# Decay, forget and write-strength rows from sixteen cumulated rows and a 0/1 product, rectifier on ScalarE

## The chip, the cores and the metric

The kernel runs on one core of one Trainium2 chip. The metric is the device time of one execution in microseconds (us), the median of several runs. A time in a trace is counted from the start of the profiled execution's span. PE is TensorE, DVE VectorE, ACT ScalarE, POOL GpSimd, and SP the engine that issues the weight loads.

## What is computed

Two transformer blocks for 256 tokens of width 1024, one after the other. The change lies in the second one, whose mixer has four heads of a gated delta rule (GDN, head size 128) and eight heads of a "forgetting" attention (FoX). Cut to what matters:

```python
proj = rmsnorm(h) @ w_in
g_qkv, g_z, g_a, g_b, f_qkv, f_f = split(proj)
g_qkv = silu(causal_depthwise_conv(g_qkv, conv_w))       # 12 tiles of 128 features: q, k, v of 4 heads
gq, gk = l2norm(gq), l2norm(gk)
beta = sigmoid(g_b)                                      # write strength, (tokens, 4)
g_decay = -exp(a_log) * softplus(g_a + dt_bias)          # log decay, (tokens, 4)
# gated_delta_rule, by chunks:
gc = cumsum(g_decay)
decay = where(lower, exp(gc[i] - gc[j]), 0)
a_mat = where(strict, (k * beta) @ k.T * decay, 0) + eye # then a triangular solve
# forgetting_attention:
log_f = log_sigmoid(f_f + fox_f_bias)                    # (tokens, 8)
c = cumsum(log_f)
logits = q @ k.T * scale + c[i] - c[j]                   # causal softmax over j, times v
```

## The kernel before

**Tiling and weights.** Every large product is made of three products of fp32r parts (high times high, high times low, low times high). Weights stream in groups of 1 MB through a ring of three: SP loads `raw`, ACT rounds it to `w_hi` (`hi_until`, L668), DVE subtracts to `w_lo` (`lo_until`, L1275), PE uses both. A group of the ring is rounded when PE has used the group three before it. Each engine has its own instruction stream, written out by hand in the order in which it runs, and the streams meet in counting semaphores: `wait_ge` on one of them holds everything behind it on that engine.

**The stage of the change.** For j = 0 to 5, `gdn_tiles(j)` on PE makes two tiles of 128 features for 256 tokens (48 matmuls of 256 columns). ACT moves them out of PSUM with the middle tap (`gdn_mid`, L987), DVE adds the other three taps (`gdn`, L1668, six instructions), ACT does the silu (`gdn_silu`, L995), PE turns four heads at a time to tokens (`to_tokens`, L2112). Tiles 0 and 1 are the queries, 2 and 3 the keys, 4 and 5 the values. ACT squares the turned rows (`token_squares`, L1017), DVE sums them, POOL makes the root (L605, L606) and DVE the normed `qk_n` (`token_norms`, L1711). PE turns these back (`gT`, moved out by ACT, L1066) and forms the products kk of keys with keys and queries (L2562).

**What the change touches.** DVE makes `g_dec`, `beta` and `lf2` (log forget) for each token (L1687 to L1694). PE then has, behind `gdn_tiles(2)`:

- `decay_sums` (L2483): the cumulated decay `gc` as columns (L2488, L2489), and for each of 2 token tiles and 4 heads a 128x128 product of the head's `g_dec`, broadcast as the stationary operand, with the triangle `s_le_t` (L2492). Each gives the cumulated row, the same on all partitions.
- `forget_sums(i)` (L2496), i = 0 to 3, each for two of the eight FoX heads: six such 128x128 products into bank 7 (L2506 to L2508), moved out negated to `neg_c` by ACT's `fsum_out(i)` (L1009). All these products are plain fp32.
- behind the flips of `qk_n`: eight products that spread `beta` over the partitions (L2552).

DVE subtracts `gc` from the decay rows and cuts at zero (`decT`, L1723, eight instructions), ACT takes the exponential (L1040). `egc` (L1729, L1043) holds exponentials of `gc` columns. DVE multiplies kk by `decT` and by the spread `beta` to `cT` (L1748, L1751), and the triangular solve starts from `cT`.

## Time and profile before

| | us |
|---|---|
| median of 3 runs | 809.65 |
| lowest, highest | 808.44, 810.8 |
| profiled execution | 811.04 |
| its span (first to last instruction) | 809.1 |
| PE busy in the span | 776.0 (96%) |
| DVE busy | 540.3 (67%) |
| ACT busy | 414.6 (51%) |
| POOL busy | 93.3 (12%) |

How to read it: a busy share is an average over stages. A row of the timeline gives the start, the length of the merged instructions, the engine, the line of the kernel, the operation and its tiles, how many instructions it merges, and in brackets the time that the engine sat idle before it and who ended that. A matmul's length includes its way through the array, so matmuls overlap: what one costs PE is the distance between starts. A plain fp32 matmul shows as two entries (x16 for eight).

### The profile page before, as it was taken

Reading aid. Unit: us, or ns where it says so; the run is one execution under the profiler, and the core shown is the slowest. Engines: PE = TensorE matmul, PEld = TensorE weight load, DVE = VectorE, ACT = ScalarE, POOL = GpSimd, SP = SyncE. Lnnn points to the kernel's source line nnn. Section 1 sums busy time; section 2 is a strip of 40 time slices with the busy share of each in tenths; the row PEclk is TensorE's granted clock in tenths of the full one; section 3 lists DMA queues with packets and bytes.
Section 4 is the critical chain, followed back from the end, with each engine's and each line's share of the span. In section 5 each row is a group of like instructions: output and inputs, shape, how many; then the busy total and the mean of one; then the engine's idle time right before and its main releaser. Section 6 shows DMA issues by size and latency. Waiting matters only on the chain. (4 is left out here: it accounts for less than half of the span.)

```text
span 809.1 us, 11764 instructions
## 1 busy us (share of the span) xinstructions
PE 776.0 (96%) x4591; PEld 665.5 (82%) x4591; DVE 540.3 (67%) x713; ACT 414.6 (51%) x581; POOL 93.3 (12%) x154
## 2 busy tenths in 40 slices
PE   4899999999999999999989999999999999999996
PEld 3777877777889899888889988988788898988884
DVE  0676789876777888877577885564466666654365
ACT  2632422634676776634267545556365454543364
POOL 3100401311200000000170313210100000000000
PEclk9999999999999999999999999999999999999998
DMA  9976576814276555588454343312465555545711
GB/s 307 362 251 222 196 247 228 301 54 143 79 234 207 184 176 181 188 275 301 150 141 150 104 157 103 105 55 66 143 233 173 192 193 172 206 157 185 232 53 53
DMA packets 107900, 144.83 MB, mean 179 GB/s; under 512 B 6343, under 2 KB 70352, under 8 KB 107856
## 3 DMA queue, kind: packets, MB, share of 16 engines
q1 hardware_dynamic: 100512, 137.38, 51.1%
q10 hardware_dynamic: 7280, 6.83, 2.7%
q8 instruction: 30, 0.49, 0.2%
q14 instruction: 14, 0.11, 0.0%
q0 software_dynamic: 64, 0.01, 0.0%
HBM read 142.10 MB, written 2.10 MB: 178 GB/s over the span
## 5 line engine op out<-in xcount | busy, mean ns | idle before, releaser
L2072 PE MATMUL ps<-h_parts,w_hi 128*128 128x512 f32 x504 | 179.6, 396 | 0.0
L1275 DVE TENSOR_TENSOR w_lo<-raw,w_hi 128x2048 fp32r<-128x2048 f32 (+1 forms) x61 | 135.6, 2230 | 63.4 <-ACT w_hi L668 63.2
L668 ACT CAST w_hi<-raw 128x2048 fp32r<-128x2048 f32 (+1 forms) x61 | 112.9, 1852 | 80.6 <-PE ps L1948 56.8
L2071 PE MATMUL ps<-h_parts,w_lo 128*128 128x256 f32 x504 | 140.5, 279 | 0.0
L1283 DVE TENSOR_TENSOR w_lo<-raw,w_hi 128x2048 fp32r<-128x2048 f32 x44 | 100.7, 2290 | 16.2 <-ACT w_hi L676 15.7
L2072 PEld LDWEIGHTS ps<-h_parts,w_hi 128*128 128x128 f32 x504 | 94.6, 188 | 19.4
L2071 PEld LDWEIGHTS ps<-h_parts,w_lo 128*128 128x128 f32 x504 | 95.0, 189 | 3.3
L676 ACT CAST w_hi<-raw 128x2048 fp32r<-128x2048 f32 x44 | 84.0, 1909 | 0.0
L1946 PE MATMUL ps<-w_hi,act_hi 128*128 128x512 f32 x176 | 69.0, 392 | 0.0
L1948 PE MATMUL ps<-w_hi,act_lo 128*128 128x512 f32 x176 | 68.5, 389 | 0.0
L1947 PE MATMUL ps<-w_lo,act_hi 128*128 128x512 f32 x176 | 68.5, 389 | 0.0
L1946 PE MATMUL ps<-w_hi,h_parts 128*128 128x512 f32 x160 | 64.2, 401 | 1.2 <-DVE h_parts L1301 0.7
L1948 PE MATMUL ps<-w_hi,h_parts 128*128 128x512 f32 x160 | 62.4, 390 | 0.0
L1947 PE MATMUL ps<-w_lo,h_parts 128*128 128x512 f32 x160 | 62.3, 390 | 0.0
L1946 PE MATMUL ps<-h_parts,w_hi 128*128 128x256 f32 x144 | 41.4, 287 | 0.0
L1947 PE MATMUL ps<-h_parts,w_hi 128*128 128x256 f32 x144 | 40.7, 283 | 0.0
L1948 PE MATMUL ps<-h_parts,w_lo 128*128 128x256 f32 x144 | 40.7, 283 | 0.0
L1947 PEld LDWEIGHTS ps<-w_lo,act_hi 128*128 128x128 f32 x176 | 33.0, 188 | 7.1 <-issue 0.2
L1946 PEld LDWEIGHTS ps<-w_hi,act_hi 128*128 128x128 f32 x176 | 33.0, 188 | 6.9 <-issue 0.2
L1948 PEld LDWEIGHTS ps<-w_hi,act_lo 128*128 128x128 f32 x176 | 33.0, 188 | 6.9
L1946 PEld LDWEIGHTS ps<-w_hi,h_parts 128*128 128x128 f32 x160 | 30.0, 188 | 9.6 <-DVE h_parts L1301 1.6
L498 POOL TENSOR_SCALAR ss<-ss 128x1 f32<-128x1 f32 x14 | 5.5, 396 | 278.4 <-ACT junk L686 278.4
(418 smaller groups left out, 1548.7 us busy)
## 6 DMA issues: line engine op xcount, KB each, us to landing
raw<-in_ffn_up_w SPq DMA_DIRECT2D x22, 1024.0 KB, 5.1
raw<-in_w_gate_up SPq DMA_DIRECT2D x22, 1024.0 KB, 5.1
raw<-in_ada_w SPq DMA_DIRECT2D x16, 1024.0 KB, 5.2
raw<-in_w_in SPq DMA_DIRECT2D x14, 1024.0 KB, 5.3
raw<-in_m_in_w SPq DMA_DIRECT2D x11, 1024.0 KB, 5.2
raw<-in_ffn_down_w SPq DMA_DIRECT2D x10, 1024.0 KB, 5.2
raw<-in_w_down SPq DMA_DIRECT2D x10, 1024.0 KB, 5.0
raw<-in_m_out_w SPq DMA_DIRECT2D x4, 1024.0 KB, 5.2
```

The lines of the kernel that those rows point to most:

```text
L498: link(pool.tensor_scalar(s, s, ss[:, c0 + TT:c0 + TT + 1], EPS, ALU.add, ALU.add))
L668: act.copy(part_view(w_hi, s), raw_view(split[s])).then_inc(hi_ready, 1)
L676: act.copy(part_view(w_hi, s), raw_view(split[s])).then_inc(hi_ready, 1)
L1275: dve.tensor_tensor(part_view(w_lo, s), raw_view(split[s]), part_view(w_hi, s).bitcast(F32), ALU.subtract).then_inc(lo_ready, 1)
L1283: dve.tensor_tensor(part_view(w_lo, s), raw_view(split[s]), part_view(w_hi, s).bitcast(F32), ALU.subtract).then_inc(lo_ready, 1)
L1946: pe.matmul(dst, l_hi, r_hi, start=first, stop=False)
L1947: pe.matmul(dst, l_hi, r_lo, start=False, stop=False)
L1948: return pe.matmul(dst, l_lo, r_hi, start=False, stop=last)
L2071: pe.matmul(both[:, 0], lo[:, k, w], h_hi[:, k, :], start=False, stop=False)
L2072: ins = pe.matmul(both, hi[:, k, w], h_parts[:, :, k, :], start=False, stop=k == KD - 1)
```

## The change

The three gates of a token become one tile of sixteen columns, `token_gates`: eight of log forget, four of decay, four of beta. `gate_sums` cumulates all sixteen at once with the columns as the stationary operand, so that they come out as sixteen rows over 256 tokens (3 products), and turns the same columns without cumulating them (2 transposes), into 16 partitions of bank 7. ACT copies these rows to fp32r (`gate_sum` 0 to 15), DVE subtracts to the rest of the rounding (`gate_sum` 32 to 47), in the memory of `mw`, which is not used any more by then. A row is spread over the 128 partitions by `spread`: a 0/1 column of `pick`, broadcast as the stationary operand, with `gate_sum`, one fp32r product of 256 columns. `decay_spread` (four, and the two of forget group 0) stands in the middle of `gdn_tiles(3)`, the other forget groups and beta where they were. The bank layout of the decay and beta rows changes from one bank for each token tile to two heads in each bank. The subtraction of `gc` and the cut at zero move from DVE to ACT as a rectifier of `gc` minus the row; the exponential takes it with the scale −1. `fsum_out(1)` moves up on ACT, `gdn(2)` on DVE stands now ahead of the wait for `egc_exp`, and DVE gains a copy of `fold` to `pick`.

ACT, from the move of gdn 2's tiles out of PSUM on (`r<-ps,cols`); before:

```order
L987 ACTIVATE r<-ps,cols 128x256 x2
L710 COPY p_out<-ps 128x512 x2
L712 DMA out<-p_out 128x2x512
L1040 ACT_TABLE_LOAD
L1040 ACTIVATE decT<-decT 128x512 x2
L1043 ACTIVATE egc<-egc 128x4 x2
L995 ACT_TABLE_LOAD
L995 ACTIVATE r<-r 128x256 x4
L1009 ACTIVATE neg_c<-ps 128x512
L668 CAST w_hi<-raw 128x2048
```

and now (here L991 is gdn_mid, L999 the silu, L1013 neg_c, L672 w_hi):

```order
L991 ACTIVATE r<-ps,cols 128x256 x2
L1041 CAST mw<-ps 16x512
L714 COPY p_out<-ps 128x512 x2
L716 DMA out<-p_out 128x2x512
L1047 ACTIVATE decT<-ps,gc 128x128 x8
L1053 ACT_TABLE_LOAD
L1053 ACTIVATE decT<-decT 128x512 x2
L1056 ACTIVATE egc<-egc 128x4 x2
L999 ACT_TABLE_LOAD
L999 ACTIVATE r<-r 128x256 x4
L1013 ACTIVATE neg_c<-ps 128x512
L672 CAST w_hi<-raw 128x2048
```

The copy of the rows and the eight rectifiers are new; the table load for the exponential stands behind the rectifiers.

PE, behind the last matmuls of gdn 2's tiles, with the first of gdn 3's; before:

```order
L1948 MATMUL ps<-h_parts,w_lo 128x256
L2488 MATMUL ps<-g_dec,s_le_t 128x4 x2
L2489 MATMUL ps<-g_dec,ones 128x4
L2492 MATMUL ps<-s_le_t,g_dec 128x128 x8
L2506 MATMUL ps<-s_le_t,lf 128x128
L2507 MATMUL ps<-ones,lf 128x128
L2508 MATMUL ps<-s_le_t,lf 128x128
L2506 MATMUL ps<-s_le_t,lf 128x128
L2507 MATMUL ps<-ones,lf 128x128
L2508 MATMUL ps<-s_le_t,lf 128x128
L1946 MATMUL ps<-h_parts,w_hi 128x256
```

and now, with, in the middle of gdn 3's tiles, the spreads (`ps<-mw,pick`):

```order
L1958 MATMUL ps<-h_parts,w_lo 128x256
L2501 MATMUL ps<-token_gates,s_le_t 128x4 x2
L2502 MATMUL ps<-token_gates,ones 128x4
L2505 MATMUL ps<-s_le_t,token_gates 16x128 x2
L2506 MATMUL ps<-ones,token_gates 8x128
L2122 MATMUL ps<-ident,token_gates 16x128 x2
L1956 MATMUL ps<-h_parts,w_hi 128x256
...
L1958 MATMUL ps<-h_parts,w_lo 128x256
L2494 MATMUL ps<-mw,pick 128x256 x6
L1956 MATMUL ps<-h_parts,w_hi 128x256
```

Fourteen products of 128 columns gave way to five, and six spreads moved into the tiles.

The diff:

```diff
         mw = sb(ctx, "mw", [64, 2, 2, T], F32R)
+        pick = sb(ctx, "pick", [64, 16], F32R)
+        gate_sum = mw[:, 0].rearrange("p d t -> p (d t)")
...
             gprm = sb(b2, "gprm", [P, 16])
-            g_dec = sb(b2, "g_dec", [P, TT, GH])
-            beta = sb(b2, "beta", [P, TT, GH])
-            lf2 = sb(b2, "lf2", [P, TT, FH])
+            token_gates = sb(b2, "token_gates", [P, TT, 16])
+            lf2, g_dec, beta = (token_gates[:, :, c0:c1] for c0, c1 in ((0, FH), (FH, FH + GH), (FH + GH, 16)))
             sp2 = sb(b2, "sp2", [P, TT, 16])
...
             return j % 2 if j >= 2 else 6 + j
+
+        def by_head_and_tile(b):
+            return ps[:, b:b + 2, :].rearrange("p b (u t n) -> p (b u) t n", u=2, t=TT)
...
             gdn_mid(2, ahead=False)
+            act.wait_ge(S("sgate_ready"), 3)
+            act.copy(gate_sum[0:16], ps[0:16, 7, :]).then_inc(S("sgate_ready"), 1)
             p_store(1)
+            act.wait_ge(S("egc_diff"), 2)
+            act.wait_ge(S("decay_mm"), 2)
+            for t in range(TT):
+                for h in range(GH):
+                    ins = act.activation(decT[:, GH * t + h, :], by_head_and_tile(5)[:, h, t, :], ACT.Relu, scale=-1.0,
+                                         bias=gc[:, t, h:h + 1])
+                ins.then_inc(S("dec_z"), 1)
             for t in range(TT):
...
                 d = decT[:, GH * t:GH * (t + 1), :]
-                act.activation(d, d, ACT.Exp).then_inc(S("dec_exp"), 1)
+                act.activation(d, d, ACT.Exp, scale=-1.0).then_inc(S("dec_exp"), 1)
             act.wait_ge(S("egc_diff"), 2)
...
             gdn_mid(3)
+            fsum_out(1)
             gdn_silu(3)
...
             token_squares(1)
-            fsum_out(1)
             gdn_mid(4, ahead=False)
...
+            dve.wait_ge(S("const_ready"), 3)
+            link(dve.tensor_copy(pick[:], fold[0:64]))
             gdn(1)
...
             dve.tensor_tensor(egc[:, 2, :], gc[:, 2, :], gc[:, 0, :], ALU.subtract).then_inc(S("egc_diff"), 1)
-            for t in range(TT):
-                dve.wait_ge(S("decay_mm"), 1 + t + 1)
-                for h in range(GH):
-                    ins = dve.tensor_scalar(decT[:, GH * t + h, :], ps[:, 5 + t, h * P:(h + 1) * P], gc[:, t, h:h + 1], 0.0,
-                                            ALU.subtract, ALU.min)
-                    if h < GH - 1:
-                        link(ins)
-                ins.then_inc(S("dec_z"), 1)
+            dve.wait_ge(S("sgate_ready"), 4)
+            dve.tensor_tensor(gate_sum[32:48], ps[0:16, 7, :], gate_sum[0:16].bitcast(F32), ALU.subtract).then_inc(S("sgate_ready"), 1)
+            gdn(2)
             dve.wait_ge(S("egc_exp"), 2)
             dve.tensor_tensor(egc[:, 1, :], egc[:, 0, :], beta[:, 1, :], ALU.mult).then_inc(S("egc_ready"), 1)
-            gdn(2)
             gdn(3)
...
                 link(dve.tensor_tensor(all_heads(cT, t), bank(4 + t), all_heads(decT, t), ALU.mult))
+            dve.wait_ge(S("beta_mm"), 1)
             for t in range(TT):
-                dve.wait_ge(S("beta_mm"), t + 1)
-                dve.tensor_tensor(all_heads(cT, t), all_heads(cT, t), bank(2 + t), ALU.mult).then_inc(S("cT_full"), 1)
+                dve.tensor_tensor(all_heads(cT, t), all_heads(cT, t), by_head_and_tile(2)[:, :, t, :], ALU.mult)\
+                    .then_inc(S("cT_full"), 1)
...
-            def decay_sums():
-
-                pe.wait_ge(S("sgate_ready"), 1)
+            def spread(dst, c, rows):
+                return pe.matmul(dst, pick[:, c:c + 1].to_broadcast([64, P]), rows, start=True, stop=True)
+
+            def gate_sums():
+
+                pe.wait_ge(S("sgate_ready"), 2)
                 pe.wait_ge(S("conv2_done"), 2)
...
                 pe.matmul(ps[:, 4, 8:12], ones[:], g_dec[:, 0, :], start=True, stop=True).then_inc(S("decay_mm"), 1)
+                pe.wait_ge(S("conv2_done"), 4)
                 for t in range(TT):
-                    for h in range(GH):
-                        ins = pe.matmul(ps[:, 5 + t, h * P:(h + 1) * P], g_dec[:, t, h:h + 1].to_broadcast([P, P]),
-                                        s_le_t[:], start=True, stop=True)
-                    ins.then_inc(S("decay_mm"), 1)
-
-            def forget_sums(i):
-
-                if i == 0:
-                    pe.wait_ge(S("sgate_ready"), 2)
-                    pe.wait_ge(S("conv2_done"), 4)
-                else:
+                    pe.matmul(ps[0:16, 7, t * P:(t + 1) * P], token_gates[:, t, :], s_le_t[:], start=True, stop=t == 0)
+                pe.matmul(ps[0:FH, 7, P:T], lf2[:, 0, :], ones[:], start=False, stop=True)
+                for t in range(TT):
+                    ins = flip(ps[0:16, 7, T + t * P:T + (t + 1) * P], token_gates[:, t, :])
+                ins.then_inc(S("sgate_ready"), 1)
+
+            def decay_spread():
+
+                pe.wait_ge(S("sgate_ready"), 5)
+                for h in range(GH):
+                    ins = spread(ps[:, 5 + h // 2, h % 2 * T:(h % 2 + 1) * T], FH + h, gate_sum[:, 0:T])
+                ins.then_inc(S("decay_mm"), 1)
+                forget_spread(0)
+
+            def forget_spread(i):
+
+                if i:
                     pe.wait_ge(S("neg_c_out"), i)
                 for b in range(2):
-                    f0, f1 = (lf2[:, t, 2 * i + b:2 * i + b + 1].to_broadcast([P, P]) for t in range(TT))
-                    c = b * T
-                    pe.matmul(ps[:, 7, c:c + P], f0, s_le_t[:], start=True, stop=True)
-                    pe.matmul(ps[:, 7, c + P:c + T], f0, ones[:], start=True, stop=False)
-                    ins = pe.matmul(ps[:, 7, c + P:c + T], f1, s_le_t[:], start=False, stop=True)
+                    ins = spread(ps[:, 7, b * T:(b + 1) * T], 2 * i + b, gate_sum[:, 0:T])
                 ins.then_inc(S("fsum_mm"), 1)
...
             gdn_tiles(2)
-            decay_sums()
-            forget_sums(0)
-            gdn_tiles(3)
+            gate_sums()
+            gdn_tiles(3, between=decay_spread)
             pe.wait_ge(S("dec_z"), TT)
...
             to_tokens(0, 1, TOKEN_BANKS[1])
-            forget_sums(1)
+            forget_spread(1)
             gdn_tiles(4)
-            forget_sums(2)
+            forget_spread(2)
             to_tokens(1, 0, TOKEN_BANKS[2])
...
             to_tokens(1, 1, TOKEN_BANKS[3])
-            forget_sums(3)
+            forget_spread(3)
             gdn_tiles(5)
...
-            for t in range(TT):
-                for h in range(GH):
-                    ins = pe.matmul(ps[:, 2 + t, h * P:(h + 1) * P], beta[:, t, h:h + 1].to_broadcast([P, P]), ident[:],
-                                    start=True, stop=True)
-                ins.then_inc(S("beta_mm"), 1)
+            for h in range(GH):
+                ins = spread(ps[:, 2 + h // 2, h % 2 * T:(h % 2 + 1) * T], FH + GH + h, gate_sum[:, T:2 * T])
+            ins.then_inc(S("beta_mm"), 1)
             fox_tiles(0)
```

## Rows read from the trace of the kernel before

**Rows 1.** The page: busy us (share of the span) x instructions of each engine.

```profile
PE 776.0 (96%) x4591; PEld 665.5 (82%) x4591; DVE 540.3 (67%) x713; ACT 414.6 (51%) x581; POOL 93.3 (12%) x154
```

**Rows 2.** Timeline of PE, 424 to 454.5 us: start, length, engine, line, operation.

```profile
431.92 0.51 PE L2488 MATMUL ps<-g_dec,s_le_t 128*128 128x4 f32 x4
...
432.51 2.03 PE L2492 MATMUL ps<-s_le_t,g_dec 128*128 128x128 f32 x16
434.38 0.39 PE L2506 MATMUL ps<-s_le_t,lf 128*128 128x128 f32 x2
...
435.64 0.36 PE L1946 MATMUL ps<-h_parts,w_hi 128*128 128x256 f32 x1
...
441.56 1.06 PE L2112 MATMUL ps<-ident,r 128*128 128x128 f32 x8
...
443.72 0.36 PE L1946 MATMUL ps<-h_parts,w_hi 128*128 128x256 f32 x1
...
450.83 0.49 PE L2506 MATMUL ps<-s_le_t,lf 128*128 128x128 f32 x2 [1.12 <-ACT neg_c L1009]
```

**Rows 3.** Timeline of ACT, 424 to 492 us.

```profile
434.39 1.28 ACT L1040 ACT_TABLE_LOAD   x1 [0.46 <-ACT p_out L710]
436.53 0.63 ACT L1040 ACTIVATE decT<-decT 128x512 f32<-128x512 f32 x1 [0.86 <-DVE decT L1723]
437.95 0.63 ACT L1040 ACTIVATE decT<-decT 128x512 f32<-128x512 f32 x1 [0.78 <-DVE decT L1723]
438.48 0.28 ACT L1043 ACTIVATE egc<-egc 128x4 f32<-128x4 f32 x2
438.79 1.28 ACT L995 ACT_TABLE_LOAD   x1
440.08 1.34 ACT L995 ACTIVATE r<-r 128x256 f32<-128x256 f32 x4
441.32 0.58 ACT L1009 ACTIVATE neg_c<-ps 128x512 f32<-128x512 f32 x1
441.80 1.89 ACT L668 CAST w_hi<-raw 128x2048 fp32r<-128x2048 f32 x1
...
468.13 2.03 ACT L1066 COPY gT<-ps 128x512 f32<-128x512 f32 x4
```

**Rows 4.** Timeline of DVE, 424 to 492 us.

```profile
429.58 2.95 DVE L1668 SCALAR_TENSOR_TENSOR r<-ps,cols,r 128x255 f32<-128x255 f32 x6 [0.27 <-ACT r L987]
...
434.99 2.92 DVE L1723 TENSOR_SCALAR decT<-ps,gc 128x128 f32<-128x128 f32 x8
...
443.72 2.29 DVE L1275 TENSOR_TENSOR w_lo<-raw,w_hi 128x2048 fp32r<-128x2048 f32 x1 [1.90 <-ACT w_hi L668]
445.93 2.94 DVE L1668 SCALAR_TENSOR_TENSOR r<-ps,cols,r 128x255 f32<-128x255 f32 x6
...
459.17 0.69 DVE L1711 TENSOR_TENSOR qk_n<-ps,rstd 128x512 f32<-128x512 f32 x1 [0.68 <-POOL rstd L606]
...
464.83 2.94 DVE L1668 SCALAR_TENSOR_TENSOR r<-ps,cols,r 128x255 f32<-128x255 f32 x6
```

**Rows 5.** Timeline of PE, 454.5 to 492 us.

```profile
460.32 1.91 PE L2112 MATMUL ps<-ident,qk_n 128*128 128x128 f32 x16
462.07 1.95 PE L2552 MATMUL ps<-ident,beta 128*128 128x128 f32 x16
...
470.21 3.84 PE L2562 MATMUL ps<-gT 128*128 128x128 f32 x32 [0.45 <-ACT gT L1066]
...
484.95 0.50 PE L1946 MATMUL ps<-w_hi,h_parts 128*128 128x512 f32 x1 [0.48 <-DVE vb L1766]
```

**Rows 6.** Timeline of ACT, 775 to 787 us.

```profile
775.76 2.17 ACT L1204 ACTIVATE h_parts<-ps,cols 128x128 fp32r<-128x128 f32 x8
```

**Rows 7.** Busy time by stretch at the end, with the granted clock (PEclk, 1.00 is 2.4 GHz).

```profile
803.00:804.00 1.00, 0.00 (x0) 0.00 (x0) 0.97 (x2) 0.60 (x2) 0.00 (x0) 1.00 0.17 62
804.00:805.00 1.00, 0.00 (x0) 0.00 (x0) 0.10 (x1) 0.12 (x2) 0.69 (x2) 0.65 0.00 0
```


## What I predict before the changed kernel runs

> **What bounds the kernel now.** I read first the page's busy shares [rows 1]: PE is busy 96% of the span. A reader who stops there will credit every removed matmul in full. So I read next, in time order, what each engine does between 430 and 485 us, where all of the change lies.
>
> PE [rows 2]: behind the tiles of gdn 2 it computes the decay sums and four groups of "forget" sums without a gap. But it meets its operands very closely. It starts the turned keys and queries (L2112) at 441.56, and the silu that makes them ends between 440.08 and 441.4 on ACT [rows 3]. It starts the flips of qk_n at 460.32 [rows 5], and the last qk_n is made by 459.86 on DVE [rows 4]. It waits 0.45 us for gT at 470.21 and 0.48 us for vb at 484.95 [rows 5]. So in this stage PE and the pair ACT and DVE run side by side with about 0.1 to 0.5 us between them: the end follows whichever is later.
>
> ACT [rows 3]: waits for decT from DVE at 436.53 and 437.95, two Exps, a table load, four Silus, one neg_c, and at 441.80 the high part of weight group 5 (w_hi, L668, 1.89 us). DVE [rows 4] waits for exactly this: 1.90 us idle before 443.72. From there DVE goes on almost by itself: low part, convolution 3 (445.93), the norms, ending in qk_n at 459.86, convolutions 4 and 5 (464.83), and ACT's gT (468.13), on which PE waits at 470.21. Its own gaps on the way are waits on POOL for rstd, which starts from DVE's own sums. So this chain is rigid: what delays w_hi 5 delays kk at 470.21, and all that follows.
>
> **The change part by part, in the time of the profiled execution** (811.04 us, span 809.1; the median of the three runs is 809.65, 1.39 lower; I carry the shift over to it unchanged).
>
> PE, removed: eight decay products, 432.51 to 434.38, 1.87 us; four forget groups of six, each 434.38 to 435.64 and some 0.08 more before the stride is back to normal, 1.34 us each, 5.4 in all; eight beta products, 1.8 [rows 2, 5]. Together 9.0 us. Added: three products of 128 moving columns at the 0.225 of the forget products (1.34/6) and two transposes at 0.11 (eight from 441.56 to 442.46), 0.9 us; sixteen spreads of 256 columns, which are of the type and width of the tiles' matmuls: 48 of these fill 435.64 to 441.56, 0.123 each, 2.0 us. Also removed is the wait of 1.12 at 450.83, since fsum_out(1) moves ahead. So PE has 6.1 us less work and up to 1.1 less waiting. That is the tempting sum: 809.65 − 7.2 = 802.4. It needs PE to be the bound all along.
>
> ACT, the new path. The three gc products still end at 432.51. The rows' products then wait for both convolutions of gdn 1, on DVE from 429.58 for 2.95 [rows 4]: 432.6. With 0.9 of products, gdn 3's tiles start at 433.5 (before: 435.64). The pick copy on DVE (64x16) falls into the 0.27 us that DVE idles before 429.58 and costs nothing; without this cover it costs its 0.17. ACT copies the sums (16x512; neg_c, a copy of 128x512, takes 0.5) at 433.6, then p_out and its DMA issue, as before with room to spare (they were through at 434.36, when gdn 2's tiles had ended at 432), and is idle by 436. DVE's subtraction (0.69, as qk_n's at 459.17) starts where decT started, 434.99, and ends at 435.7. PE comes to the spreads after half of gdn 3's tiles, 433.5 + 24 x 0.123 = 436.45, so neither is late, by 0.7 us. Four decay spreads and the drain: 437.15. This is where ACT's wait ends, and behind that wait everything else of ACT is queued.
>
> From 437.15: eight rectifiers of 128x128 from PSUM with an operand per partition. Nearest row: eight of this size with a scale per partition in 2.17 us, 0.27 each [rows 6]. Bounds: the two 128x4 Exps of 0.28 together [rows 3] with the slope of larger ones give some 0.2 each; DVE's own price for this work, 2.92 for eight, 0.365 each [rows 4]. So 1.6 to 2.9, and I take 2.2, ending at 439.35. Then the table load, 1.28: in the kernel before it was issued at 434.39 and lay under the wait for decT; now it stands behind the rectifiers, whose result the Exp wants: 440.65. Two Exps (0.63, overlapping) 441.8; egc 442.0; table load 443.3; four Silus (440.07 to 441.32 before, 1.25) 444.55; neg_c 0.48: w_hi 5 starts at 445.05, against 441.80 [rows 3]. **ACT is 3.25 us late**. DVE loses its 2.92 us of decT and does convolution 2 early, but only waits the longer for w_hi 5: nothing of that saving is on this path.
>
> DVE then starts w_lo 5 at 446.95 instead of 443.72, adds egc·beta (0.16), now ahead of convolution 3: +3.4. On the rigid chain this gives qk_n at 463.3, gT and kk at 473.6 instead of 470.21. The beta saving (1.3 us) falls into PE's wait for gT and is lost.
>
> PE, checked on this timetable: it finishes gdn 3's tiles and spreads at 440.15 and then waits for the Silus until 444.55, 4.4 us. It starts gdn 4 at 445.75 (before 443.72), ends at 451.6, waits about 1 us for silu 3 (449.3 before, 452.9 now), ends gdn 5 at 461 and waits 2.2 us for qk_n. The 7.2 us come back as these waits and that for gT. **Sum: +3.4 us**, 812.5 of span, 814.4 in a profiled execution, 813.05 on the median. With the bounds of the rectifiers (−0.6, +0.7) and some 0.3 on the spreads and semaphores: 812.1 to 814.1.
>
> Two rules of the pages beside that. Eight rectifiers took 0.365 each on DVE [rows 4] and should take 0.27 on ACT [rows 6]; the Trainium skill, page ScalarE: Activation LUTs, section Rules for kernel authors, says to put relu on VectorE and not on ScalarE. Per instruction this case's rows don't bear it out; what costs here is the queue that they stand in. Its section What ACT_TABLE_LOAD costs gives, besides the 1.28, 1.38 us of drain for each switch; in the trace the load at 438.79 starts 0.03 us after the end of egc's Exps, and the Silus follow it [rows 3]. I see no drain; with one the load now on the path would add 1.4, 814.4. It also says that cheap functions such as relu are in every set, which agrees with the order of the new kernel, where no load stands ahead of the rectifiers.
>
> **The rivals.**
> Faster: the late chain finds slack that I don't see, and PE's work sets the end. Then PE counts +2.0 at gdn 4, −1.1 and −1.1 for forget groups 2 and 3, −1.1 for the wait at 450.83 and −1.3 for beta: −2.6, 807.05. It speaks for it that PE did not wait at 460.32. It decides once the chain from 443.72 to 470.21 can shorten by 6 us; DVE's gaps on it are waits on POOL, and gT was already late by 0.45 [rows 5].
> Same: ACT's path costs a microsecond less than summed (rectifiers at their lower bound, and shorter gaps at the semaphores): +2.3 or less, 811.9 at most and 810.5 as its middle. The rows give 0.6 of that.
> Clock: PE stands still for 4.4 us. At the end of the program its last matmul ends at 801.3, the granted clock is 1.00 in 803 to 804 and 0.65 in 804 to 805 [rows 7], on its way from 2.4 to 1.2 GHz. If it falls in the new stall, gdn 4's tiles take up to 11.8 us instead of 5.9; about 3 us of PE's later waits absorb most of that. Only if gdn 5's are slow as well does convolution 5 start late, by 3.5: up to 816.5, middle 815.3. The Trainium skill, page TensorE: Matmul & The Clock Gate, section Why this matters for your kernels, warns of the clock's fall in idle gaps between bursts of matmuls; no stall of the stage before is long enough to show it.
>
> **How the numbers follow.** Forecast 0.65; same 0.18; PE sets the end, faster, 0.09; clock 0.08. What a measurement can tell from no change is 0.3%, 2.4 us. Slower by more: 0.65 + 0.08 = 0.73; within: 0.18; faster by more: 0.09. The predicted time is 813.0. From 809.3, below most of the "same" case, to 815.5, the middle of the clock case and a little more, the range leaves out the faster case, 0.04 of "same" and 0.04 at the top.
>
> **What would show it.** Right: the tiles of gdn 3 start at 433.5; eight rectifiers from about 437.2; a table load behind them; w_hi 5 at 445; PE idle for over 4 us until about 444.5 on a Silu, idle again before the flips of qk_n; kk at 473.6. Wrong in size: rectifiers far from 0.27 each. Wrong in kind: kk at 470 or earlier although w_hi 5 is late, which means the chain had slack; or ACT waiting not on the spreads but on DVE's subtraction.

## The result, and the profile after

| us | before | after |
|---|---|---|
| median | 809.49 (4 runs) | 816.84 (4 runs) |
| lowest, highest | 808.44, 810.8 | 816.33, 817.23 |
| profiled execution | 811.04 | 817.23 |
| its span | 809.1 | 815.3 |

The ratio is 1.0086, 95% interval 1.0064 to 1.0108: slower by 7.35 us, where 3.4 was forecast and 815.5 was the top of the range. The direction was right, the size was not. (One run of the kernel before among those of the experiments took 1565.39 us; it is left out of every ratio.)

The page of after, against [rows 1]: PE has 56 instructions fewer and is busy exactly as long as before.

```profile
span 815.3 us, 11656 instructions
...
PE 776.0 (95%) x4535; PEld 659.7 (81%) x4535; DVE 538.3 (66%) x707; ACT 417.1 (51%) x590; POOL 93.1 (11%) x154
```

**Where the time came from.** I paired the same instructions of the two traces and read how much later each one starts in after. Starts of the subtractions to `w_lo` on DVE (L1275 before, L1288 after):

| | before | after | later by |
|---|---|---|---|
| behind the start of the program | 120.03 | 119.13 | −0.90 |
| start of the program's first down projection | 358.82 | 358.36 | −0.46 |
| behind it | 415.85 | 416.85 | +1.00 |
| w_lo 5, in the changed stage | 443.72 | 447.92 | +4.20 |
| in the second down projection, early | 728.28 | 733.12 | +4.84 |
| late | 775.89 | 782.13 | +6.24 |

ACT moves gdn 2's tiles out at 432.12 before and 432.82 after, 0.70 later, so 3.5 us come from the changed stage, about as forecast. The rest grows slowly in two places that the diff doesn't touch: the two down projections, 264 matmuls of 512 columns each. From 120 us on after loses 7.1 us in all (0.90 and the 6.2 by which its span is longer), which agrees with the medians' 7.35. The spans differ by 6.2 only because the profiled execution of before was 0.90 slower in its start, in code that is the same in both. Starts differ from one execution to the next (by up to 4 us in the traces below), and the granted clock is a part of it: here it fell in before and not in after. Stretch, length, busy us and count of PE, PEld (weight load), DVE, ACT and POOL, then the granted clock (1.00 is 2.4 GHz) and the DMA's share and GB/s, before and then after:

```profile
74.00:78.00 4.00, 4.00 (x17) 2.70 (x16) 1.75 (x6) 0.44 (x1) 0.00 (x0) 0.59 0.19 52
```

```profile
74.00:78.00 4.00, 4.00 (x23) 3.13 (x22) 3.40 (x7) 0.00 (x0) 0.00 (x0) 1.00 0.05 15
```

Single executions are therefore compared from 120 us on in what follows.

**The changed stage.** ACT of after, 424 to 500 us (start, length, engine, line, operation; answers to [rows 3]):

```profile
434.55 0.58 ACT L1041 CAST mw<-ps 16x512 fp32r<-16x512 f32 x1 [0.89 <-PE ps L2122]
435.03 1.05 ACT L714 COPY p_out<-ps 128x512 f32<-128x512 f32 x2
...
438.14 2.17 ACT L1047 ACTIVATE decT<-ps,gc 128x128 f32<-128x128 f32 x8 [2.07 <-PE ps L2494]
440.33 1.28 ACT L1053 ACT_TABLE_LOAD   x1
441.63 1.15 ACT L1053 ACTIVATE decT<-decT 128x512 f32<-128x512 f32 x2
442.68 0.28 ACT L1056 ACTIVATE egc<-egc 128x4 f32<-128x4 f32 x2
442.98 1.28 ACT L999 ACT_TABLE_LOAD   x1
444.28 1.33 ACT L999 ACTIVATE r<-r 128x256 f32<-128x256 f32 x4
445.52 0.57 ACT L1013 ACTIVATE neg_c<-ps 128x512 f32<-128x512 f32 x1
446.00 1.89 ACT L672 CAST w_hi<-raw 128x2048 fp32r<-128x2048 f32 x1
```

ACT waits 2.07 us for the spreads (L2494), makes eight rectifiers in 2.17, and only then loads the table. DVE, same stretch (answers to [rows 4]), makes convolution 2 at once and then sits idle for 8.37 us until w_hi 5:

```profile
435.89 0.68 DVE L1736 TENSOR_TENSOR mw<-ps,mw 16x512 fp32r<-16x512 f32 x1
436.60 2.94 DVE L1681 SCALAR_TENSOR_TENSOR r<-ps,cols,r 128x255 f32<-128x255 f32 x6
447.92 2.29 DVE L1288 TENSOR_TENSOR w_lo<-raw,w_hi 128x2048 fp32r<-128x2048 f32 x1 [8.37 <-ACT w_hi L672]
...
463.43 0.69 DVE L1724 TENSOR_TENSOR qk_n<-ps,rstd 128x512 f32<-128x512 f32 x1 [0.68 <-POOL rstd L610]
```

PE, its timeline (answers to [rows 2, 5]); the saved work is there as waits, in the brackets:

```profile
434.27 0.36 PE L1956 MATMUL ps<-h_parts,w_hi 128*128 128x256 f32 x1
...
437.31 0.98 PE L2494 MATMUL ps<-mw,pick 64*128 64x256 f32 x6
438.22 0.39 PE L1956 MATMUL ps<-h_parts,w_hi 128*128 128x256 f32 x1
...
445.76 1.94 PE L2122 MATMUL ps<-ident,r 128*128 128x128 f32 x8 [4.40 <-ACT r L999]
...
464.18 1.97 PE L2122 MATMUL ps<-ident,qk_n 128*128 128x128 f32 x16 [1.11 <-DVE qk_n L1724]
...
474.46 3.84 PE L2575 MATMUL ps<-gT 128*128 128x128 f32 x32 [1.42 <-ACT gT L1079]
```

**The down projections.** Groups by line of PE over 722 to 782 us (count, busy us, mean ns of one), before and then after. In a down projection the activations are the stationary operand and `w_hi` or `w_lo` the moving one.

```profile
L1947 PE MATMUL ps<-w_lo,act_hi 128*128 128x512 f32 x78 | 30.4, 389 | 0.0
```

```profile
L1957 PE MATMUL ps<-w_lo,act_hi 128*128 128x512 f32 x83 | 32.8, 396 | 0.0
```

Each matmul takes 7 ns more at a granted clock of 1.00. The mean distance between the starts of neighbours, worked out from the timeline rows of both down projections, went from 0.2268 to 0.2333 us: 528 x 0.0065 = 3.4 us. The same view over 560 to 600 us, after, separates two stationary operands that go through the same lines:

```profile
L1958 PE MATMUL ps<-w_hi,fox_lo 128*128 128x512 f32 x16 | 6.3, 395 | 0.0
...
L1958 PE MATMUL ps<-w_hi,h_parts 128*128 128x512 f32 x16 | 6.2, 390 | 0.0
```

Before, both stood at 390; the FoX matmuls add some 0.25 us to the 3.4. `h_parts` is allocated ahead of the new tensor `pick`; `fox_hi`, `fox_lo`, `act_hi`, `act_lo` and `act2_hi`, `act2_lo` behind it. `pick` is 16 fp32r columns, 64 bytes of each partition, and moves all of them by 64 bytes.

### The profile page after: what moved, and what is told of

Its sections match the earlier page's. It is cut to its first block and busy times, and to the rows that moved or that the text cites. A ratio compares the mean times of both kernels' runs of the same rounds, so it can differ in the third digit from the quotient of the medians.

```text
span 815.3 us, 11656 instructions
## 1 busy us (share of the span) xinstructions
PE 776.0 (95%) x4535; PEld 659.7 (81%) x4535; DVE 538.3 (66%) x707; ACT 417.1 (51%) x590; POOL 93.1 (11%) x154
## 5 line engine op out<-in xcount | busy, mean ns | idle before, releaser
L1288 DVE TENSOR_TENSOR w_lo<-raw,w_hi 128x2048 fp32r<-128x2048 f32 (+1 forms) x61 | 135.4, 2225 | 73.9 <-ACT w_hi L672 73.7
L672 ACT CAST w_hi<-raw 128x2048 fp32r<-128x2048 f32 (+1 forms) x61 | 113.0, 1852 | 84.9 <-PE ps L1958 62.1
```

The costliest lines, as they stand in the source:

```text
L672: act.copy(part_view(w_hi, s), raw_view(split[s])).then_inc(hi_ready, 1)
L1288: dve.tensor_tensor(part_view(w_lo, s), raw_view(split[s]), part_view(w_hi, s).bitcast(F32), ALU.subtract).then_inc(lo_ready, 1)
```

## Experiments on the address

Theory: 3.5 us come from the 64 bytes, 3.5 from ACT's path. Rival: the down projections are slow for another reason that came with the change (the clock, weight transfers), and `pick` has no part in it. Ratios are against runs of the kernel before on the same chip.

**Undone: `pick` in memory that is free by then.** The rest of the change stays.

```diff
-        pick = sb(ctx, "pick", [64, 16], F32R)
+        pick = mw[:, 1, 0, 0:16]
```

> The changed kernel with one edit: pick is no tensor of its own (64 bytes in each partition, allocated ahead of act_hi, act_lo and all of the second block) but lies in the unused half of mw, so that every other tensor has the address it had in the kernel before. Theory A (two causes: the stage between 430 and 490 us costs 3.5 us, and the shifted addresses of the stationary operands slow the two down stages, whose matmuls stand 0.2335 us apart instead of 0.2267, 528 of them, 3.6 us): the down stages return to 0.2267, and the time is 3.6 us below the changed kernel's 816.8, about 813.2. Rival B (the slower stride comes from something else, such as the length or position of PE's program or the clock after the new stall): the stride stays 0.2335 and the time stays within 1 us of 816.8.

Measured: 813.68 us (811.31 to 816.1), ratio 1.0040 (1.0020 to 1.0060). The same group is back at its old length, and the distance at 0.2268:

```profile
L1957 PE MATMUL ps<-w_lo,act_hi 128*128 128x512 f32 x79 | 30.7, 389 | 0.0
```

The same kernel once more, to see how far that time can be trusted:

> The kernel of e1_pick_in_mw once more, since its runs spread over 5 us. If the stage alone is left of the change (3.5 us in the traces): 809.0 + 3.5 = 812.5 against the kernel before on the same chip. If something costs beyond that which the traces of the stage don't show: 813.5 or more.

Measured: 814.15 us (811.9 to 816.46), 1.0048 (1.0027 to 1.0069), more than expected. The two together give 1.0044, so undoing this line takes 0.0042 from the change's 1.0086, 3.4 us; the intervals are wide enough for 1 to 6. The traces say it more closely: from 120 us to the end after takes 696.14 us, e1 692.49 and before 689.05. Undoing the line gives back 3.65, the two down projections and the FoX matmuls; what is left, 3.44, is the changed stage. (The whole span of e1, 809.4, is only 0.3 above that of before, because its start ran 3.2 us faster, over the same code.) Why e11's profiled span is 3.1 above e1's is read below.

**Alone: the kernel before, with 64 unused bytes.** Nothing reads or writes the tensor.

```diff
         mw = sb(ctx, "mw", [64, 2, 2, T], F32R)
+        unused = sb(ctx, "unused", [64, 16], F32R)
```

> The kernel before with one tensor more that nothing uses, 64 bytes in each partition, in the place where the changed kernel has pick. Theory A (addresses): the 528 matmuls of the two down stages stand 0.2335 us apart instead of 0.2267, and the time is 809.5 + 3.6 = 813.1. Rival B (not the addresses): 809.5, stride 0.2267.

Measured: 815.99 us (812.98 to 818.57, 8 runs), 1.0067 (1.0041 to 1.0093). An unused tensor alone makes the kernel slower, which fells the rival. The distance between starts is 0.2334 in both down projections and the group of act_hi has the length of after:

```profile
L1948 PE MATMUL ps<-w_lo,act_hi 128*128 128x512 f32 x79 | 31.2, 396 | 0.0
```

The median moved by 6.7 us, more than the 3.65 that these and the FoX matmuls explain. The interval reaches down to 3.3 us, and its trace takes 3.9 us more than that of before from 120 us on, with a fall of the clock at 410 in it. What the other 2.8 us of the median are isn't shown.

**Only one down projection at a time.** The same 64 bytes directly ahead of `act_hi` in the scope of the first, or of `act2_hi` in that of the second:

```diff
             with ExitStack() as fs:
+                unused = sb(fs, "unused", [64, 16], F32R)
                 act_hi = sb(fs, "act_hi", [P, KF, T], F32R)
```

> The kernel before with 64 unused bytes in each partition directly ahead of act_hi and act_lo of the first block's down stage alone; the second block's act2_hi and act2_lo keep their addresses. Theory A (the address of the stationary operand against that of the weights sets the stride): 0.2335 us between matmuls in the first down stage and 0.2267 in the second, and 1.8 us more than the kernel before, 810.8 where before stands at 809.0. Rival A3 (it is another tensor that moved along in the 64-byte kernels, or the program): both stages at 0.2267 or both at 0.2335.

> The kernel before with 64 unused bytes directly ahead of act2_hi and act2_lo of the second block's down stage alone. Theory A: stride 0.2267 us in the first down stage, 0.2335 in the second, 1.8 us more than the kernel before. Rival A3: both stages alike.

Measured: 811.19 us, 1.0013 (0.9996 to 1.0030), for the first; 812.66, 1.0031 (1.0012 to 1.0050), for the second. Distances: 0.2333 and 0.2267 for the first kernel, 0.2269 and 0.2333 for the second. Groups of the first kernel over 350 to 392 and over 722 to 782 us, then of the second over the same stretches:

```profile
L1949 PE MATMUL ps<-w_hi,act_lo 128*128 128x512 f32 x58 | 22.9, 395 | 0.0
...
L1949 PE MATMUL ps<-w_hi,act_lo 128*128 128x512 f32 x82 | 31.9, 389 | 0.0
```

```profile
L1949 PE MATMUL ps<-w_hi,act_lo 128*128 128x512 f32 x60 | 23.4, 389 | 0.0
...
L1949 PE MATMUL ps<-w_hi,act_lo 128*128 128x512 f32 x80 | 31.6, 395 | 0.0
```

Only the projection whose stationary operand moved is slower, 264 x 0.0065 = 1.7 us; the moving operand (`w_hi`, `w_lo`, allocated ahead of all of this) stayed where it was in every kernel here. The first kernel's median alone can't be told from no change, the distances can.

**Other sizes**, at the place of `pick`: 128 and 256 bytes.

> As e2_pad64 (the kernel before and a tensor that nothing uses), but with 128 bytes in each partition instead of 64. Theory A1 (it is the alignment of the stationary operands act_hi and act_lo that matters: 64 bytes shift them by half a step of 128, 128 bytes by a whole one): the stride of the down stages stays 0.2267 us and the time equals the kernel before, 809.3. Rival A2 (any shift of these operands costs, or something else that moved with them): 0.2335 and some 3.6 us more, as with 64 bytes.

> As e2_pad64 and e2_pad128, with 256 unused bytes in each partition. With 64 the matmuls of the down stages took 0.2335 us, with 128 about as much. If the pattern has a period of up to 256 bytes: 0.2267 and no more than the kernel before, 809.0. If any shift off the present addresses costs: 0.233 and about 812.3.

Measured: 811.86 us, 1.0029 (1.0013 to 1.0046), with 128 bytes, distances 0.2324; 808.88, 1.0005 (0.9987 to 1.0023), with 256 bytes, distances 0.2268. Group over 722 to 782 us, 128 bytes and then 256:

```profile
L1948 PE MATMUL ps<-w_lo,act_hi 128*128 128x512 f32 x79 | 31.2, 395 | 0.0
```

```profile
L1948 PE MATMUL ps<-w_lo,act_hi 128*128 128x512 f32 x80 | 31.1, 389 | 0.0
```

So it is not the amount of memory but where the operand starts: at 0 and 256 bytes from the old place it is fast, at 64 and 128 slow. Other offsets weren't tried. The theory that 128 bytes would be as good as none was wrong.

## Experiments on ACT's path

These build on e1, so their comparison is 813.68 and 814.15, not 816.84. Theory: what costs is that w_hi 5 stands in ACT's stream behind the wait for the spreads, the rectifiers and the table load. Rivals: the PE's stall of 4.4 us itself, by way of the clock; or the rectifiers' price on ACT.

**The cut back on DVE**, ahead of `gdn(2)`, the exponential without its scale:

```diff
-                    ins = act.activation(decT[:, GH * t + h, :], by_head_and_tile(5)[:, h, t, :], ACT.Relu, scale=-1.0,
-                                         bias=gc[:, t, h:h + 1])
...
+                    ins = dve.tensor_scalar(decT[:, GH * t + h, :], by_head_and_tile(5)[:, h, t, :], gc[:, t, h:h + 1], 0.0,
+                                            ALU.subtract, ALU.min)
```

> As e1_pick_in_mw, but the subtraction of gc and the cut at zero stay on DVE (eight tensor_scalar, ahead of gdn(2), as in the kernel before), with the exponential's scale +1 again. Theory A (the late w_hi 5 is ACT's rectifiers plus the table load that no longer lies under a wait): the table load is hidden again and the second tile's cut overlaps the first one's exponential; the cuts end at about 440.8, w_hi 5 starts at about 44.7 + 400 = 444.7 against 446.0 in the changed kernel (in before 441.8), and the time is some 1.2 us below e1_pick_in_mw, 812.0. Rival C (it matters little where the cut is made, what is late are the spreads in the middle of gdn 3's tiles): within 0.4 us of e1_pick_in_mw.

Measured: 812.40 us, 1.0031 (1.0011 to 1.0051). On the profile ACT reaches w_hi 5 12.00 us after it moves gdn 2's tiles out, against 13.14 in e1, 13.18 in after and 9.68 before. Its table load is under the wait again, at 434.68:

```profile
434.68 1.28 ACT L1046 ACT_TABLE_LOAD   x1 [0.46 <-ACT p_out L714]
437.78 0.63 ACT L1046 ACTIVATE decT<-decT 128x512 f32<-128x512 f32 x1 [1.81 <-DVE decT L1733]
```

So of the 3.5 us by which w_hi 5 is late, the rectifiers' place on ACT, with the table load behind it, makes 1.1. The other 2.3 are there in e3 too, where the rows still come later (ACT's copy, DVE's subtraction, and spreads in mid-tile); these were not taken apart. The products kk start 40.47 us behind that same move (the entry, from here on) in e3 and 41.59 in e1, so the 1.1 reach it. The medians of e1 and e3 differ by 1.3, within their intervals.

**Only the table load early.** One extra exponential of a single column, whose result nobody reads, ahead of the wait:

```diff
             p_store(1)
+            act.activation(early_exp, ones[:, 0:1], ACT.Exp)
             act.wait_ge(S("egc_diff"), 2)
```

> As e1_pick_in_mw, with one Exp of a single column of ones ahead of ACT's wait for the spreads, whose result nothing uses: its table load, 1.28 us, then lies under that wait (2.07 us idle), and none stands behind the rectifiers. Theory A: w_hi 5 starts 1.3 us earlier and the time is 1.3 us below e1_pick_in_mw, about 811.9. Rival C (the table load is not on the path that sets the end): no change against e1_pick_in_mw.

Measured: 813.03 us, 1.0041 (1.0021 to 1.0060). ACT did gain 1.37 (w_hi 5 after 11.77 us), and the last qk_n comes 1.35 us earlier behind the entry than in e1. But in the profiled execution PE now waited 1.91 us for qk_n, and the granted clock fell after it. Timeline and clock by stretch (columns as in the section on the result):

```profile
459.73 2.88 PE L2124 MATMUL ps<-ident,qk_n 128*128 128x128 f32 x16 [1.91 <-DVE qk_n L1726]
...
460.00:464.00 4.00, 4.00 (x21) 3.44 (x20) 3.86 (x7) 1.86 (x5) 0.79 (x1) 0.58 0.02 4
464.00:468.00 4.00, 4.00 (x22) 4.00 (x22) 3.86 (x8) 2.30 (x4) 0.00 (x0) 0.57 0.51 145
```

The flips took 2.88 instead of 1.97 and the tiles behind them ran at little over half speed. PE did not wait for gT any more; kk starts 41.41 us behind the entry, against 41.59, so the fall took back 1.2 of the 1.35. This is the mechanism of the clock rival, at another place than I had it: PE without slack behind it, so that slow tiles count. Whether every timed run had this fall isn't known: the median is 0.65 below e1's, the lowest run 0.97 below e1's lowest, and 1.3 was expected.

**PE kept busy in its stall.** 36 extra matmuls into a free bank, of no use to the result, ahead of PE's wait:

```diff
+            pe.wait_ge(S("conv2_done"), 6)
+            for i in range(36):
+                pe.matmul(ps[:, 0, 0:T], h_hi[:, i % KD, 0:P], h_hi[:, i % KD, :], start=True, stop=True)
             pe.wait_ge(S("dec_z"), TT)
```

> As e1_pick_in_mw, with 36 matmuls of 256 columns into a free bank, whose result nothing uses, where PE stands still for 4.4 us before the turned queries, so that it doesn't. It tells what the fall of the clock costs. Theory A (PE has room of some 3 us behind the stall, so the slow stretch is absorbed): granted clock 1.00 throughout the stage, the 8 transposes take 1.06 us instead of 1.94, and the time is within 0.5 us of e1_pick_in_mw. Rival D (the clock is part of the loss): 1.5 us or more below it.

Measured: 813.38 us, 1.0050 (1.0033 to 1.0066), no better than e1. In after the clock does fall in the stall:

```profile
440.00:444.00 4.00, 1.35 (x12) 1.15 (x10) 0.00 (x0) 3.95 (x8) 0.00 (x0) 0.93 0.51 189
444.00:448.00 4.00, 2.24 (x9) 1.94 (x10) 0.08 (x1) 3.99 (x8) 0.00 (x0) 0.50 0.01 4
448.00:452.00 4.00, 4.00 (x25) 3.78 (x25) 3.93 (x6) 3.77 (x7) 0.00 (x0) 0.71 0.17 20
```

With the filler it is 1.00 through 436 to 448, and the eight transposes take 1.06 instead of 1.94. Then it falls later, at 452 to 460 (0.65 and 0.93). So the filler moved the fall and did not do away with it. What it shows is that the fall in the stall is absorbed, as reckoned: with it gone, kk starts 41.65 us behind the entry (41.59 in e1), and DVE's chain from w_lo 5 on has the same waits.

**w_hi 5 ahead of the wait.** One line moved up on ACT, everything else as in e1:

```diff
             p_store(1)
+            hi_until(at["gdn"][2] + 4)
             act.wait_ge(S("egc_diff"), 2)
```

> As e1_pick_in_mw, but ACT rounds weight group 5 before it waits for the spreads (there it idles 2.07 us, and the rounding takes 1.89). Theory A (what passes the lateness on is DVE's wait for w_hi 5): DVE makes w_lo 5 behind convolution 2 without a wait, convolution 3 then waits for ACT's move of gdn 3's tiles and starts about 2.2 us earlier than in e1_pick_in_mw; the time is some 2 us lower, 811.7. Rival D (what passes it on is PE's wait for the Silus, with the clock that falls in it): PE's 4.4 us stall is as long as before, and the time stays within 0.5 us of e1_pick_in_mw's 813.7.

Measured: 809.61 us, 1.0005 (0.9988 to 1.0022): by the medians level with the kernel before and 4.1 us below e1. By the traces a part of the loss stays: from the move of gdn 2's tiles to w_lo 9 (the subtraction at 472.48 before) e5 takes 41.37 us, before 40.36 and e1 43.85, so 2.5 of the 3.5 are gone. From 120 us on it takes 1.3 more than before, and its lowest run is 1.3 above the lowest of before, which the interval allows. PE's stall is longer than ever, 4.7 us, and the clock still falls with it (0.92 and 0.65 in 440 to 448):

```profile
433.47 1.91 ACT L672 CAST w_hi<-raw 128x2048 fp32r<-128x2048 f32 x1 [0.53 <-ACT p_out L714]
435.28 2.17 ACT L1048 ACTIVATE decT<-ps,gc 128x128 f32<-128x128 f32 x8
...
444.60 2.94 DVE L1682 SCALAR_TENSOR_TENSOR r<-ps,cols,r 128x255 f32<-128x255 f32 x6 [4.31 <-ACT r L991]
```

This decides between the theory and the stall: the stall stays and most of the loss is gone. What cost most was the place of w_hi 5 in ACT's stream. Convolution 3 on DVE now waits 4.31 us for the next thing that is queued on ACT, the move of gdn 3's tiles, and starts 1.0 us later behind the entry than before; that is the part that stays.

**ACT's stream in a new order.** w_hi 5 and the first silus ahead of the rectifiers, the exponentials of the decay behind the squares (they are needed only at `cT`), with POOL's and DVE's uses of them moved along:

```diff
-            p_store(1)
+            hi_until(at["gdn"][2] + 4)
+            gdn_silu(0)
+            gdn_silu(1)
             act.wait_ge(S("egc_diff"), 2)
...
             fsum_out(0)
-            hi_until(at["gdn"][2] + 4)
+            gdn_mid(3, ahead=False)
             gdn_silu(2)
-            gdn_mid(3)
+            p_store(1)
+            hi_until(at["gdn"][3] + 4)
...
             fsum_out(3)
+            for t in range(TT):
+                act.wait_ge(S("dec_z"), t + 1)
+                d = decT[:, GH * t:GH * (t + 1), :]
+                act.activation(d, d, ACT.Exp, scale=-1.0).then_inc(S("dec_exp"), 1)
```

> As e1_pick_in_mw with ACT's order rearranged around the new row products: weight group 5, the Silus 0 and 1, the rectifiers, neg_c 0, gdn_mid(3), Silu 2, p_store, group 6 and so on, and the exponentials of decT with their table load only behind group 7; POOL takes its cut of decT behind all four rstd, DVE forms egc*beta behind convolution 4. Nothing else changes. Theory A (the work saved on PE is real, and ACT's queue alone hid it): PE does not wait for the Silus, convolution 3 starts about 4 us earlier than in the kernel before, kk at 470.2 - 4 in its time, and the whole takes about 805.5. Rival D (the chain through DVE and POOL from the norms to gT is tight in any order): no faster than the kernel before, 809.3.

Measured: 807.42 us (806.33 to 810.24), 0.9973 (0.9955 to 0.9990): faster than both kernels, by 2.2 us against the kernel before (0.8 to 3.6), though not the 805.5 that was expected. PE meets the turned queries almost without a wait:

```profile
span 805.5 us, 11657 instructions
...
439.66 1.09 PE L2123 MATMUL ps<-ident,r 128*128 128x128 f32 x8 [0.33 <-ACT decT L1049]
440.68 0.50 PE L2495 MATMUL ps<-mw 64*128 64x256 f32 x2
...
449.71 0.50 PE L2495 MATMUL ps<-mw 64*128 64x256 f32 x2 [1.13 <-ACT neg_c L1013]
```

The granted clock stays at 1.00 from 436 to 476. From the move of gdn 2's tiles to w_lo 9 it takes 38.14 us, against 40.36 before and 43.85 in e1. So 2.2 of PE's 6.1 us can be had once neither `pick` nor ACT's queue takes them back; 1.5 still goes into the wait for gT and 1.1 into that for neg_c. Convolution 3 does start 3.75 us earlier than before, as expected, but kk only 2.2. In between DVE waits 1.06 us for a w_hi and 0.84 for the squares, and both stand on ACT behind `p_store`, which the new order had moved there; by the trace the squares wait 1.43 us for its transfer:

```profile
447.36 1.09 ACT L1021 ACTIVATE r<-ps 128x512 f32<-128x512 f32 x2 [1.43 <-DMA out<-p_out]
```

**All traces from 120 us on.** The time from the same subtraction to `w_lo` (120.03 in before) to the end of the span, how much more that is than before, and where the granted clock fell on the way:

| | from 120 us on | more than before | clock fell at |
|---|---|---|---|
| before | 689.05 | | |
| after | 696.14 | 7.09 | 443 |
| e1 | 692.49 | 3.44 | 439 |
| e11, the same kernel | 695.29 | 6.24 | 408, 442, 487 |
| e2_pad64 | 692.98 | 3.93 | 410 |
| e2_pad128 | 693.61 | 4.56 | 409, 484 |
| e10_pad256 | 689.11 | 0.06 | |
| e8_pad_first | 691.16 | 2.11 | 411 |
| e9_pad_second | 690.92 | 1.87 | 411 |
| e3_dve_rect | 692.59 | 3.54 | 409, 443 |
| e4_table_early | 692.88 | 3.83 | 461 |
| e5_w5_early | 690.34 | 1.29 | 443 |
| e6_pe_filler | 692.63 | 3.58 | 453 |
| e7_order | 686.82 | −2.23 | |

Where a kernel's matmuls and stage explain less than its row (e2_pad128: 528 x 0.0056 = 3.0 of 4.56), the falls stand beside it; what each of them cost was read only for e4 and e11.

**What another fall of the clock costs.** e11 is e1, 3.1 us longer in the profiled span. It is 0.3 later at 120 us. At 408 its clock falls, behind a wait of PE of 2.37 us that e1 has too (2.35) without a fall (0.57 against 1.00 in 408 to 412), and it enters the changed stage 1.50 late (gate products at 430.23 against 428.73); so that fall makes 1.2. It passes the stage equally fast. Then, with the same waits at 484, the clock falls in e11 and not in e1. Stretches of e11, then of e1:

```profile
484.00:488.00 4.00, 2.54 (x11) 1.89 (x12) 4.00 (x6) 1.75 (x4) 0.00 (x0) 0.86 0.01 2
488.00:492.00 4.00, 4.00 (x14) 3.18 (x13) 2.98 (x6) 0.00 (x0) 2.03 (x3) 0.71 0.47 131
```

```profile
484.00:488.00 4.00, 3.39 (x16) 2.73 (x17) 4.00 (x5) 0.71 (x2) 0.00 (x0) 1.00 0.00 0
488.00:492.00 4.00, 4.00 (x25) 3.49 (x24) 2.59 (x4) 0.68 (x2) 3.54 (x4) 1.00 0.80 261
```

From the flips of q_exp to the products on L2670 e11 needs 8.27 us (485.64 to 493.91), e1 6.67 (484.14 to 490.81): 1.6 us for one fall where PE is the bound. 0.3, 1.2 and 1.6 are the 3.1 us. Such a fall is as large as the differences between e1, e3, e4 and e6, so those are not told apart by their times, only by their traces.

## The prediction, step by step

- **Tiles of gdn 3 at 433.5, spreads, rectifiers at 437.15.** Right. After runs 0.7 us late on entering the stage (gdn 2's tiles are out at 432.82, before at 432.12, from the first down projection); less that, tiles 433.57 and rectifiers 437.44. The sixteen spreads were put at 0.123 each; six in a row moved the next tile by 0.91 us, 0.15 each, and two in a row by 0.44, 0.22 each. The sum had them too cheap, by 0.17 us for the six and by about as much again for each pair.
- **Rectifiers 0.27 each.** Right to the hundredth: eight in 2.17, as [rows 6].
- **The table load comes on the path.** Right, 440.33 to 441.61, directly behind the rectifiers. The Trainium skill's page ScalarE: Activation LUTs, section What ACT_TABLE_LOAD costs, would add 1.38 us of drain. The rectifiers end at 440.31, the load starts 0.02 later and the Exp follows at 441.63; e4 took the load off the path and gained 1.37. No drain shows, the measurement decides.
- **w_hi 5 late by 3.25, w_lo 5 by 3.4.** Right: relative to the entry 445.30 and 3.5.
- **The rigid chain hands on the whole delay.** Right: qk_n, gT and kk are 4.25 late, 0.7 of it from the entry. kk starts at 474.46; 473.6 was said, 473.76 is what it makes less the 0.7.
- **PE's waits.** The first was said to be 4.4 us and is 4.40; before the flips 2.2 was said and 1.1 seen; in e4, where the clock had not fallen by then, it is 1.91, so the slow stretch filled most of the rest. None of PE's 6.1 us reached the end.
- **The clock rival.** The clock fell in the new stall, which I gave 0.08, but the fall was absorbed, as that rival's own arithmetic allowed. That the measured 816.84 lies near its upper end of 816.5 is chance: kk is 3.55 late with the fall in, and the rest came elsewhere. In the variants the clock fell at other, dearer places (e4, e11), which I had not priced.
- **The sum.** This is the step that failed. "The pick copy on DVE (64x16) falls into the 0.27 us that DVE idles" prices the instruction on `pick` and nothing else of it. The tensor is the new line in the allocation, it shifts the stationary operands of 528 matmuls outside the stage, and the sum had no term for that: 3.4 us, and 0.25 more in the FoX matmuls. With it the forecast would have been 816.4, against 816.84 measured. My range rested on "between 430 and 485 us, where all of the change lies"; the diff's allocation line contradicted that, and I passed over it.

What stays open: why the stationary operand's start matters, whether it is its place or its place relative to the moving one (the moving one was never shifted), what makes up the 2.3 us of w_hi 5's lateness that e3 leaves, and why e2_pad64's median moved by 6.7 where its trace shows 3.9. The clock's falls in single executions can be part of that, and so can the start of the program, which took between 116.9 us (e1) and 120.9 (e10_pad256) up to the same subtraction, over the same code; the timed runs have no trace to show it.

## What to carry to other kernels

Read the allocations in a diff as closely as the instructions: a tensor of 64 bytes ahead of others moved every later operand, and a change of 7 ns in a matmul that occurs 528 times cost as much as all that the edit itself did. Before crediting work that is taken from the busiest engine, follow what the new dependency puts ahead of the next weight group in the helper engine's stream; moving the rounding of one weight group ahead of the wait gave back 2.5 of 3.5 us here. Compare two traces from a point behind the start of the program, and look up every fall of the clock in both, before their spans are compared: one fall, or the start, made as much as an edit here.

## What the runs showed of the hardware

- A 128x512 fp32r matmul with a 128x128 stationary operand, one behind another: 0.2268 us apart with the stationary operand at its old place or 256 bytes on, 0.2333 with 64 bytes, 0.2324 with 128. The weight load's own entry is 188 ns in both cases; the loss shows only in the matmul's.
- The granted clock fell to 1.2 GHz in waits of PE of 4.4 to 4.7 us (after, e1, e11, e5) and behind one of 1.9 in e4. A wait of 2.1 to 2.4 us that ends between 406 and 412 us, which all fourteen traces have, had a fall behind it in six of them and none in eight. The same waits of 0.4 to 0.6 us around 484 us had one in e11 and in e2_pad128 and none in e1.
- Such a fall cost nothing where PE waited again soon (e1 against e6), 1.2 us in e4 and 1.6 in e11, where PE set the end.
- The kernel before itself lay between 807.7 and 812.8 us in 35 runs on one chip, 25 of them below 809.8 and 10 above 810.9. The start of the program varied by as much between the traces, over the same code; that it makes these two groups is likely, not shown. A difference of 2 us needs its interval.
